# Expert layer of a two-block model: 96 tokens instead of 64 through gathered expert rows

## What is computed

```python
def peer(h, w_query, keys_1, keys_2, expert_u, expert_v):     # h: 512 tokens x 1024
    q = (h @ w_query).reshape(tokens, 8, 256)                 # 8 heads
    s1 = einsum('chk,nk->chn', q[..., :128], keys_1)          # 128 keys each
    s2 = einsum('chk,nk->chn', q[..., 128:], keys_2)
    v1, i1 = top_k(s1, 16); v2, i2 = top_k(s2, 16)
    cand = v1[..., :, None] + v2[..., None, :]                # 256 sums per head
    top_s, pos = top_k(cand, 16)
    experts = (i1 * 128 + i2) at pos                          # 8 x 16 = 128 picks of 16384 experts
    gate = softmax(top_s)
    act = gelu(einsum('chkd,cd->chk', expert_u[experts], h))
    return einsum('chk,chkd->cd', gate * act, expert_v[experts])
```

## Time and profile before

| | |
|---|---|
| median of three runs | 2892.67 us (2890.58 to 2893.76) |
| the profiled execution | 2894.16 us |
| its span, first to last instruction | 2892.3 us |
| TensorE matmul busy | 2834.2 us (98%) |
| TensorE weight load busy | 2434.0 us (84%) |
| VectorE busy | 1748.2 us (60%) |
| GpSimd busy | 1266.4 us (44%) |
| ScalarE busy | 1116.3 us (39%) |
| DMA moved | 532.75 MB, 184 GB/s over the span |
| mean granted TensorE clock | 0.996 |

### The profile page before, as it was taken

One profiled execution on the slowest core, in us unless ns is written; L12 is line 12 of the kernel. 1 busy time (PEld: TensorE's weight loads), 2 busy tenths in 40 slices (PEclk: granted clock), 3 DMA queues, 4 the chain that ended last, 5 costly groups with the idle time before them and its releaser, 6 DMA issues.

```text
span 2892.3 us, 42109 instructions
## 1 busy us (share of the span) xinstructions
PE 2834.2 (98%) x14606; PEld 2434.0 (84%) x14606; DVE 1748.2 (60%) x2980; ACT 1116.3 (39%) x1499; POOL 1266.4 (44%) x1348
## 2 busy tenths in 40 slices
PE   7899999999999999999999999999999999999998
PEld 5777888887688888788788999999999999999998
DVE  7958555324535542399521999577773665666664
ACT  5554222236542222423333333466564333333332
POOL 2634777646057775598554778311110121212210
PEclk9999999999999999999999999999999999999999
DMA  8315555532035555232222444688887877778872
GB/s 336 124 45 197 194 198 182 163 93 93 15 106 190 192 171 164 76 114 82 80 95 86 151 155 147 205 298 286 287 291 258 280 269 263 274 281 303 286 256 83
DMA packets 184380, 532.75 MB, mean 184 GB/s; under 512 B 17376, under 2 KB 79584, under 8 KB 182496
## 3 DMA queue, kind: packets, MB, share of 16 engines
q1 hardware_dynamic: 143584, 402.44, 41.5%
q0 software_dynamic: 18432, 67.12, 7.0%
q10 hardware_dynamic: 22272, 61.98, 5.6%
HBM read 470.65 MB, written 60.82 MB: 184 GB/s over the span
## 4 chain that ended last, share of the span: by engine, by line
PE 56%; POOL 23%; issue 18%; DVE 2%; ACT 1%; DMA 1%; POOLq 0%; ACTq 0%; DVEq 0%
PE ps L2033 42%; POOL w_lo L626 23%; PE pa L2033 14%; DVE ada L1274 0%; DMA cols<-in_cols 0%; DVE s_tmp L1803 0%; DVE mg_lo L1805 0%; DMA keys<-in_keys 0%; ACT mg_hi L1112 0%; DVE s_m L1801 0%; DVE x L1320 0%; DVE h_lo L1359 0%; DVE sq L1353 0%; POOLq L624 0%; POOLq L634 0%
## 5 line engine op out<-in xcount | busy, mean ns | idle before, releaser
L626 POOL TENSOR_TENSOR w_lo<-raw,w_hi 128x256 fp32r<-128x256 f32 x1216 | 1113.0, 948 | 725.1 <-ACT w_hi L663 724.1
L2033 PE MATMUL ps<-h_hi,w_hi 128*128 128x512 f32 (+1 forms) x2392 | 918.1, 384 | 13.6 <-ACT h_hi L758 4.0
L2033 PE MATMUL ps<-h_hi,w_lo 128*128 128x512 f32 (+1 forms) x2392 | 908.8, 380 | 0.0
L2033 PE MATMUL ps<-h_lo,w_hi 128*128 128x512 f32 (+1 forms) x2392 | 886.3, 379 | 0.0
L663 ACT ACTIVATE w_hi<-raw 128x1024 fp32r<-128x1024 f32 x509 | 539.2, 1061 | 882.5 <-PE ps L2033 629.3
L2033 PEld LDWEIGHTS ps<-h_hi,w_hi 128*128 128x128 f32 x2392 | 450.5, 188 | 89.8 <-issue 8.7
L2033 PEld LDWEIGHTS ps<-h_hi,w_lo 128*128 128x128 f32 x2392 | 450.4, 188 | 69.1 <-issue 0.2
L2033 PEld LDWEIGHTS ps<-h_lo,w_hi 128*128 128x128 f32 x2392 | 450.1, 188 | 67.8 <-issue 0.7
L1912 DVE TENSOR_TENSOR w_lo<-raw,w_hi 128x1024 fp32r<-128x1024 f32 x200 | 243.9, 1220 | 56.2 <-ACT w_hi L663 56.2
L644 POOL DMA_INDIRECT t_row<-in_u_rows,t_ix x64 | 65.4, 1021 | 470.2 <-DVE t_dot L1919 465.2
L1274 DVE CUSTOM_DVE_ANT_0 ada<-ada,cvec 128x1024 f32<-128x1024 f32 x144 | 225.9, 1598 | 29.8 <-DMA ada<-in_ada 25.2
(11 more groups left out here) (384 smaller groups left out, 3791.3 us busy)
## 6 DMA issues: line engine op xcount, KB each, us to landing
ada<-in_ada SPq DMA_DIRECT2D x144, 512.0 KB, 4.7
raw<-in_expert_u SPq DMA_DIRECT2D x128, 512.0 KB, 3.8
raw<-in_expert_v SPq DMA_DIRECT2D x128, 512.0 KB, 5.0
raw<-in_ffn_in SPq DMA_DIRECT2D x88, 512.0 KB, 4.0
expert_act<-g_act ACTq DMA_DIRECT2D x128, 224.0 KB, 4.3
gate_matrix<-w_st ACTq DMA_DIRECT2D x14, 2048.0 KB, 8.3
e_w<-gate_matrix SPq DMA_DIRECT2D x16, 1792.0 KB, 9.8
e_g<-expert_act SPq DMA_DIRECT2D x128, 224.0 KB, 6.6
```

The source lines that it names most:

```text
L626: last = nc.gpsimd.tensor_tensor(w_lo[:, k, c:c + 256], raw[:, k, c:c + 256], w_hi[:, k, c:c + 256].bitcast(F32), ALU.subtract)
L2033: return nc.tensor.matmul(out, a, b, start=start, stop=stop_)
```

## The change

96 tokens are gathered instead of 64; the dense products have 416 columns. The 64 tokens keep two picks a gather (64 gathers, `RA`), the 32 others are laid out at four picks a gather (32 gathers), with a `t_dup2`, `t_h2`, `t_sel2` and a third sum of their own. `U_FIRST` goes from 56 to 64 blocks, `U_GATES` from 56 to 52 (13 gate stages, so a half iteration of `two_stages` at the end), `U_LAST` from 16 to 12. The indices of the first 128 tokens are computed right after the router's first iteration. 18 key gathers are issued by GpSimd between its splits, behind every second block from block 20, into slots `t_early`, and their 18 dots stand behind every third step of the router from step 24. The router's loop and ScalarE's loops over `expert_v` are written out. `V_SLOTS` goes from six to five. The value rows begin at block 44 of `expert_v`; 20 dots stand in the gate part, 8 in the last `expert_u` blocks, 50 in `expert_v`. The first transposes go from behind block 52 to behind block 4, the second eight stand behind block 60.

```diff
-GT = 64
+GT, GA, GB = 96, 64, 32
 ND = S - GT
-PKS = P // GT
-ROWS = P // PKS
-U_SLOTS, V_SLOTS = 3, 6
-U_FIRST, U_GATES = 56, 56
+PA, PB = P // GA, P // GB
+RA, ROWS = P // PA, P // PA + P // PB
+U_SLOTS, V_SLOTS = 3, 5
+U_FIRST, U_GATES = 64, 52
 U_LAST = NK - U_FIRST - U_GATES
+EARLY, E_BLOCK, E_STEP = 18, 20, 24
+G_DOTS, L_DOTS, V_DOTS = 20, 8, 44
...
-        late(0, 2)
+        late(0, 6)
...
-        late(2, 3)
+        late(6, 8)
...
-            return max(0, b) * 3 // 4
+            return EARLY + max(0, b) * G_DOTS // U_GATES
         if b < U_BLOCKS:
-            return U_GATES * 3 // 4 + (b - U_GATES) // 4
-        return min(ROWS, U_GATES * 3 // 4 + U_LAST // 4 + int(front(b - U_BLOCKS) * 5 / 8))
+            return EARLY + G_DOTS + (b - U_GATES) * L_DOTS // U_LAST
+        rest = ROWS - EARLY - G_DOTS - L_DOTS
+        return ROWS - rest + min(rest, int(front(b - U_BLOCKS) * rest / (V_DOTS - 4)))
...
-        return min(ROWS, int(front(max(0, v - V_DOTS)) * 3 / 4))
+        return min(ROWS, int(max(0, front(v) - V_DOTS) * ROWS / (GE * (NG - 1) - 2 - V_DOTS)) if v > V_DOTS + 1 else 0)
...
+        pool.wait_ge(row_ready, 2)
+        for m in range(first * RING, gates):
             split(m, m % RING)
-        pool.wait_ge(row_ready, 2)
+            b = m - M0["expert_u"] - E_BLOCK
+            if b >= 0 and b % 2 == 0 and b // 2 < EARLY:
+                gather(b // 2)
+        pool.wait_ge(row_ready, 3)
         pool.wait_ge(rt_mm, 1)
-        for j in range(ROWS):
...
+        for j in range(EARLY, ROWS):
+            gather(j)
...
         four(0)
+        act.wait_ge(row_mm, 1)
+        nc.scalar.activation(t_h[:, :].rearrange("p (b n) -> p b n", b=2), pa[:, 0:2, :], ACT.Copy).then_inc(row_copied, 1)
...
         act.wait_ge(top_done, 1)
+        act.wait_ge(row_mm, 2)
+        nc.scalar.activation(t_h2[:, :].rearrange("p (b n) -> p b n", b=2), pa[:, 2:4, :], ACT.Copy).then_inc(row_copied, 1)
...
         def step(ins):
             own_d.link(dve, ins)
+            taken["steps"] += 1
+            if taken["steps"] >= E_STEP and taken["steps"] % 3 == 0 and taken["dots"] < EARLY:
+                if taken["dots"] == 0:
+                    dve.wait_ge(row_ready, 2)
+                    dve.wait_ge(row_copied, 1)
+                dve_dot(dve, taken["dots"])
+                taken["dots"] += 1
...
-        for a in range(PKS):
-            last = v.tensor_tensor(t_dup[:, :, a * GT:(a + 1) * GT], h_hi[:, :, 0:GT].bitcast(F32),
-                                   h_lo[:, :, 0:GT].bitcast(F32), ALU.add)
+        for dup, n, tok in ((t_dup2, GB, slice(GA, GT)), (t_dup, GA, slice(0, GA))):
+            for a in range(P // n):
+                last = v.tensor_tensor(dup[:, :, a * n:(a + 1) * n], h_hi[:, :, tok].bitcast(F32), h_lo[:, :, tok].bitcast(F32), ALU.add)
...
+            if i == 0:
+                for rows, tok, picks, cols_ in parts_of():
+                    last = v.scalar_tensor_tensor(out=t_dot[rows, cols_], in0=r_i[tok, 0, 0, picks], scalar=float(NK),
+                                                  in1=r_i[tok, 1, 0, picks], op0=ALU.mult, op1=ALU.add)
+                step(last)
+                v.tensor_copy(t_ix[:, :], t_dot[:, :]).then_inc(row_ready, 1)
...
                 if last:
-                    pe.wait_ge(row_ready, 3)
-                    done = mm(v_bank[k][:, 0:GT], t_sum[0][:, k * P:(k + 1) * P], t_sel[:, :], True, True)
+                    pe.wait_ge(row_ready, 4)
+                    mm(v_bank[k][:, 0:GA], t_sum[0][:, k * P:(k + 1) * P], t_sel[:, :], True, True)
+                    done = mm(v_bank[k][:, GA:GT], t_sum[2][:, k * P:(k + 1) * P], t_sel2[:, :], True, True)
```

More of the change, by code:

```diff
@@ L633, in pool_program, with gather @@
         gates = M0["expert_u"] + U_FIRST
-        with pool.Fori(2, gates // RING) as i:
+        first = (M0["expert_u"] + E_BLOCK) // RING
+        def gather(j):
+            if j >= U_SLOTS:
+                pool.wait_ge(row_used, j - U_SLOTS + 1)
+            nc.gpsimd.indirect_dma_start(out=row_slot(j)[:, :], out_offset=None, in_=A["u_rows"],
+                                         in_offset=bass.IndirectOffsetOnAxis(ap=t_ix[:, j:j + 1], axis=0))\
+              .then_inc(u_in[j % U_SLOTS], 16)
+        with pool.Fori(2, first) as i:
             for k in range(RING):
                 split(i * RING + k, k)
-        for m in range(gates // RING * RING, gates):
+        pool.wait_ge(row_ready, 2)
+        for m in range(first * RING, gates):
             split(m, m % RING)
-        pool.wait_ge(row_ready, 2)
+            b = m - M0["expert_u"] - E_BLOCK
+            if b >= 0 and b % 2 == 0 and b // 2 < EARLY:
+                gather(b // 2)
+        pool.wait_ge(row_ready, 3)
         pool.wait_ge(rt_mm, 1)
-        for j in range(ROWS):
[L642 to L646, removed]
+        for j in range(EARLY, ROWS):
+            gather(j)
         pool.wait_ge(blk_done, M0["expert_v"])
@@ L1168, in act_peer, with two_stages @@
         m, T = m + U_FIRST, T + U_FIRST
-        def two_stages(i):
-            for k in range(WPER):
+        def two_stages(i, blocks=WPER):
+            for k in range(blocks):
                 hi.loop(i, WPER, m + k)
@@ L1211, in act_peer @@
         m = M0["expert_v"]
[L1212 to L1224, removed]
+        for g in range(NG - 2):
+            for k in range(GE):
+                hi.upto(m + GE * g + k + 3)
+                wa_part(g + 1, k, (g + 1) % 2)
+                if GE * g + k == V_DOTS:
+                    act.wait_ge(row_used, ROWS)
+                    nc.scalar.activation(t_act[:, :], t_dot[:, :], ACT.Gelu_apprx_tanh).then_inc(row_copied, 1)
         for k in range(GE):
@@ L1827, in dve_top16, with parts_of @@
         settle(last)
+    def parts_of():
+        for n, tok, cols_ in ((GA, slice(0, GA), slice(0, RA)), (GB, slice(GA, GT), slice(RA, ROWS))):
+            per = cols_.stop - cols_.start
+            for a in range(P // n):
+                yield slice(a * n, (a + 1) * n), tok, slice(a * per, (a + 1) * per), cols_
     def dve_router(dve):
         v = nc.vector
+        taken = {"steps": 0, "dots": 0}
         def step(ins):
             own_d.link(dve, ins)
+            taken["steps"] += 1
[5 more added lines that the diff above has]
+                taken["dots"] += 1
         def settle(ins):
@@ L1873, in dve_router @@
         v.tensor_tensor(e, e, bc(z1, 2, TK), ALU.mult).then_inc(gate_done, 1)
+        assert taken["dots"] == EARLY
         dve.wait_ge(gate_done, 1)
[L1875 to L1881, removed]
+        for rows, tok, picks, cols_ in parts_of():
+            last = v.tensor_copy(t_gate[rows, cols_], r_i[tok, 2, 0, picks])
+        last.then_inc(row_ready, 1)
         v.tensor_copy(iota_t[:, :, :], bc(iota, 2, 2))
@@ L2449, in pe_peer @@
         m, T = M0["expert_u"], T0["expert_u"]
-        with pe.Fori(0, U_FIRST // RING - 1) as i:
-            for k in range(RING):
-                first(m, T, k, i, RING)
+        for k in range(RING):
+            first(m, T, k, 0, RING)
         pe.wait_ge(row_ready, 1)
@@ L2456, in pe_peer @@
         last.then_inc(row_mm, 1)
+        with pe.Fori(1, U_FIRST // RING - 1) as i:
+            for k in range(RING):
+                first(m, T, k, i, RING)
+        for d in range(DT):
+            last = nc.tensor.transpose(pa[:, 2 + d // 4, d % 4 * P:(d % 4 + 1) * P], t_dup2[:, d, :], ident)
+        last.then_inc(row_mm, 1)
         for k in range(U_FIRST - RING, U_FIRST - RING // 2):
@@ L2469, in pe_peer, with two_stages @@
         m, T = m + U_FIRST, T + U_FIRST
-        with pe.Fori(0, ND // WTOK // 2) as i:
-            for k in range(WPER):
+        def two_stages(i, blocks=WPER):
+            for k in range(blocks):
                 first(m, T, k, i, WPER)
@@ L2482, in pe_peer @@
                     last.then_inc(wb_mm, 1)
+        with pe.Fori(0, ND // WTOK // 2) as i:
+            two_stages(i)
+        two_stages(ND // WTOK // 2, WPER // 2)
         m, T = m + U_GATES, T + U_GATES
```

76 lines of the change are left out of this document (43 added, 33 removed).

## The result

| | before | after | forecast |
|---|---|---|---|
| time, median us | 2892.4 | 2857.8 | 2821 (2806 to 2850) |
| profiled execution, span | 2894.2, 2892.3 | 2856.8, 2854.9 | |
| expert_u stage | 680.0 | 645.7 | 640.5 |
| expert_v stage | 624.3 | 623.8 | 592 |

The ratio is 0.9887, with a 95% interval of 0.9867 to 0.9907: faster by a little over 1%, but outside the range. The stages run from TensorE's first dense product of each to the next stage's, the last to its last product; the forecasts of stages are the prediction's terms on the profiled times (680.0 - 37.8 - 3.7 + 1 + 1; 624.3 - 37.8 + 1.7 + 4). The first stage came as forecast but for 5 us. The last should have given 32 us and gave 0.5.

What follows compares the result with a forecast made beforehand. TensorE, busy throughout the expert layer, was taken as the bound. Its own sum of -76.6 us, +1 for the router and +4 for expert_v gave -71.6: 2892.7 - 71.6 = 2821 us, range 2806 to 2850.

Steps and rivals of the forecast that it cites:

- (c): Dense products: the weight load, not the columns, sets 202.7 ns; 2893 us, no change; chance 0.08.
- (b): Dense products: column slope steeper than 0.384 ns; through the origin 89 us gained instead of 75.6, 2808 us; chance 0.13.
- my 0.384: Dense products: ns a column, from 227.3 and 202.7 ns at two widths; gives 190.4 ns at 416 columns.
- The first wait: Router: VectorE waits 21 us for the first early gather before its first dot.
- the bound of +8: Router: upper bound in us if gathers land at the 10.2 us end or dots drift; +1 taken.
- The loop: expert_v: gates load after the eighth product, next products wait; 36.7 us against TensorE's 36.6; +4 us, bound +37.
- S: expert_v loop: time from a group's second product to its eighth; 20.3 us forecast.
- L: expert_v loop: time from a group's eighth product to the next group's second; 16.4 us forecast.
- the gates' product late after the boundary: expert_v: sign that the last stage is the bound, 10 us or more with TensorE idle; 6 to 8 us expected.
- rival (a): expert_v: last stage turns into the bound; +1.5 to 2.5 us in 15 groups, 2840 to 2855 us; chance 0.16.
- Rival (d): expert_v: transfers keep their mean 283 GB/s, stage 700 us instead of 622, total 2933 us; chance 0.05.
- The 2 us a group: expert_v: cost of each burst at a group's head under the 358 GB/s rule; sum +20 us instead of +4.

Runs made afterwards that it cites:

- run 2: Changed kernel with each group's gates loaded in two halves, the first already after the fourth product of the group before: 2817.2 us, ratio 0.9742.
- run 8: Changed kernel with early gathers four expert blocks sooner (E_BLOCK 16 for 20): 2850.0 us; together with gates in two halves, the first early: 2809.5 us.

## Where the prediction was right and where it failed

**Columns: right.** 190.4 ns forecast, 188.9 to 190.0 measured; the last stage without its stalls takes 583.6 us (run 2) where the terms gave 588; (c), the weight load as limit, is out, and (b) holds in part: from 202.7 down to these the slope is 0.40 to 0.43 ns a column, steeper than my 0.384. The spacing rule of the Trainium skill ("TensorE: Matmul & The Clock Gate", section "Wait - 56ns, not 53.3ns?"), would give 175.8 ns at 416 columns: its slope of 0.417 fits here, its level lies 13 ns low, as it did at 448.

**Router: mis-sized, inside its bounds.** Gates were forecast for 1861 and TensorE's demand for 1862. The kernel after, in place of the earlier trace rows:
```profile
1858.85 0.11 DVE L1904 MEMSET r_z<- 128x64 f32 x1
1862.00 0.69 DVE L1909 TENSOR_REDUCE r_z<-r_i 128x32 f32<-128x512 f32 x1 [3.03 <-ACT r_i L1178]
...
1859.00 1.03 ACT L1177 ACTIVATE t_h<-pa 128x1024 f32<-128x1024 f32 x1 [8.72 <-DVE r_z L1904]
...
1864.36 2.79 PE L2509 MATMUL pa<-consts,r_i 128*128 128x128 f32 x12 [4.64 <-DVE r_i L1911]
```
The stage began 2.8 us sooner in this execution (1574.0), in code that didn't change; over twelve profiled executions of these kernels that start lay between 1573.0 and 1578.4, so it is no gain of the change. Routing ended 284.8 us after it, 278 forecast. The first wait was over-, the rest underestimated: 17.8 us for the first dot (21 forecast), but two more such waits of 4.1 and 1.9 us, the copies and the index operations 3.7 + 4.7 us where I had 2.7 + 2.7 (each of six small index operations took 0.64 to 0.69 us), and dots of 1.42 us in the mean instead of 1.22. TensorE stood 4.6 us, then ran a few matmuls at the lower clock (347 ns). The four blocks around it took 26.6 us, against 20.0 in the kernel of run 8 with the earlier gathers: 6.6 us where I had taken +1, inside the bound of +8.

**The expert_v stage: wrong.** The loop cost 40.2 us (623.8 against 583.6 in run 2), not 4. The step that failed is the size of one term of the loop: "the wait grows by the row gathers that share the engines [...] (about 1.3 rows more at the group's head [...])", 16.4 us. S was right (20.3 against 20.6), L was 19.3. I priced the bytes by which a group's head grows, 1.2 to 1.7 us, and not how much later the load itself lands with more gathered data beside it: 9.5 us before, 13.7 after, with up to 1.28 MB in its first 9 us instead of 0.52. The place had been seen, with its signs: the gates' product late after the boundary (8 to 15 us in eight of nine groups), and it was rival (a). That was priced at 1.5 to 2.5 us a group and given 0.16; it cost 2.7, of which 0.6 is the clock that fell after the longer gaps, which no term of mine held. A loop forecast at 36.7 against 36.6 deserved better than even odds on stalling, since its error could only go one way. The range was also narrower than the bounds it was said to hold: 2892.7 - 76.6 + 1 + 37 is 2854, and 2861 with the router's +8, not 2850. The measured time lies inside those bounds, and the loop slightly beyond its own (2.7 against 2.5 us a group).

**DMA.** Rival (d) is out: 344 GB/s in the changed kernel, and 361 over 188 us at a share of 0.99 in run 2 without any harm. I cited "DMA: Bandwidth & Descriptors", section "Where 436 GB/s comes from", of the Trainium skill, for a bound of some 358 GB/s between HBM and SBUF, and held 398 in a burst against it. Over a long stretch the trace comes out close to that figure (361), in ten microseconds it doesn't; whether that bound is what holds the 361 no run here shows. The 2 us a group that I derived from it would have been nearer the truth than my 0.3, but not by its mechanism: run 2 moves the same bytes in less time and doesn't stall.

## What to carry to other kernels

Where the next load may start only when the last user of its one buffer is done, its latency stands in a loop with the steps between; compare that loop with the bound engine's period, and price the latency with all that the change adds beside it, since a loop without slack pays every microsecond, in every round. Ask then what the first user needs: half the load, or half of it early, took the loop off the path at no cost in bytes. And when a wait shows at one instruction, move that instruction first only if nothing larger stands behind it: here that moved the stall to the next block and the boundary and saved nothing.

## What I had not expected of the hardware

After a gap TensorE may come back at half its clock: its matmuls start every 347 ns instead of 189 (1.2 in place of 2.4 GHz) for 6 to 15 of them. In the last stage of the changed kernel it did so after all four gaps of 4.2 to 4.8 us, from start to start, and after one of two gaps of 2.5, and not after 0.8, 1.3, 1.8 and 3.4 us. That is a quarter of what the stalls of this stage cost. A gather's issue kept GpSimd 0.95 us in the median of the early ones and 1.68 us beside the row sums, up to 3.91; in the kernel before the median beside the row sums was 1.08. Why it grew no run here shows.
